# Attention of a diffusion trunk: two units' value products as one interleaved set, the probability copy placed first on ScalarE, filler products in two more branches

## The reference

```python
# A: two maps for each head, latent queries see 512 latent and 128 cached context keys
s = einsum(q, k) * scale ; p = softmax(s)
p = p[:, :, 0] - lam * p[:, :, 1] ; out = p @ v
# B: window of 128 around the query among the latent keys, plus 128 context keys, and a sink
p = exp(s - m) / (sum(exp(s - m)) + exp(sink - m)) ; out = p @ v
# C, D: one softmax over all 640 keys (C: 64-wide heads, D: 96-wide heads)
```

## Time and profile before

| what | us |
| --- | --- |
| median of three runs | 5234.26 |
| the profiled execution's own time | 5237.16 |
| its span | 5235.3 |
| attention of layer 1, first score product to last value product | 256 |
| PE busy in the whole span | 5096.8 (97%) |
| DVE busy | 3237.9 (62%) |
| ACT busy | 1682.5 (32%) |
| mean granted clock of PE | 0.986 |

### The profile page before, as it was taken

One profiled execution on the slowest core, in us unless ns is written; L12 is line 12 of the kernel. 1 busy time (PEld: TensorE's weight loads), 2 busy tenths in 40 slices (PEclk: granted clock), 3 DMA queues, 4 the chain that ended last, 5 costly groups with the idle time before them and its releaser, 6 DMA issues.

```text
span 5235.3 us, 68750 instructions
## 1 busy us (share of the span) xinstructions
PE 5096.8 (97%) x25730; PEld 4123.0 (79%) x25730; DVE 3237.9 (62%) x7229; ACT 1682.5 (32%) x2618; POOL 1268.3 (24%) x826
## 2 busy tenths in 40 slices
PE   7999999999999999999999999999999999999999
PEld 4666887788888888888876668868888888888887
DVE  3865211149899876666648652111698998666666
ACT  3344321333333332222233442213333333322222
POOL 1300221224434421111113002202344434111111
PEclk9989999999999999999999899999999999999999
DMA  7100121456787788888820001211577787888886
GB/s 281 34 26 1 48 73 60 189 206 220 264 282 253 246 310 290 290 290 290 288 76 29 26 1 55 70 60 61 205 253 242 268 280 238 319 289 289 289 290 222
DMA packets 349898, 982.01 MB, mean 188 GB/s; under 512 B 31648, under 2 KB 101408, under 8 KB 346272
## 3 DMA queue, kind: packets, MB, share of 16 engines
q1 hardware_dynamic: 216000, 553.19, 31.7%
q0 software_dynamic: 74880, 276.86, 15.3%
q10 hardware_dynamic: 58720, 148.04, 7.2%
HBM read 829.43 MB, written 148.54 MB: 187 GB/s over the span
## 4 chain that ended last, share of the span: by engine, by line
PE 85%; DVE 8%; DMA 2%; ACT 2%; issue 1%; DVEq 1%; ACTq 0%; POOL 0%; POOLq 0%; SPq 0%
PE PS L925 27%; PE PS L882 23%; PE PS L502 14%; PE PS L491 5%; PE PS L906 4%; PE PS L645 3%; PE PS L673 3%; DVE AR L1319 2%; PE PS L657 1%; PE PS L492 1%; PE PS L615 1%; DVE AR L1340 1%; DVE SM L1358 1%; DMA gates_by_expert<-AR 1%; PE PS L828 0%
## 5 line engine op out<-in xcount | busy, mean ns | idle before, releaser
L925 PE MATMUL PS<-HB,VR 128*128 128x512 f32 x6144 | 1394.8, 389 | 3.4 <-DVE HB L1619 3.4
L925 PEld LDWEIGHTS PS<-HB,VR 128*128 128x128 f32 x6144 | 1154.1, 188 | 244.9 <-issue 5.0
L882 PE MATMUL PS<-HR,UR 128*128 128x512 f32 x4128 | 1008.0, 398 | 0.0
L1662 POOL TENSOR_TENSOR UR<-WR,UR 128x1024 fp32r<-128x1024 f32 x212 | 529.5, 2499 | 1822.5 <-ACT UR L1125 945.7
L502 PE MATMUL PS<-HR,UR 128*128 128x320 f32 (+1 forms) x5952 | 914.2, 312 | 14.0 <-DVE HR L1294 9.7
L502 PEld LDWEIGHTS PS<-HR,UR 128*128 128x128 f32 x5952 | 877.3, 188 | 44.4 <-issue 27.4
L882 PEld LDWEIGHTS PS<-HR,UR 128*128 128x128 f32 x4128 | 764.3, 189 | 165.7
L1606 DVE TENSOR_TENSOR VR<-HT,VR 128x1024 fp32r<-128x1024 f32 x256 | 313.7, 1226 | 455.9 <-ACT VR L1244 368.1
L1244 ACT CAST VR<-HT 128x1024 fp32r<-128x1024 f32 x256 | 268.8, 1050 | 960.1 <-PE PS L925 955.9
L882 PE MATMUL PS<-HR 128*128 128x512 f32 x2016 | 486.6, 394 | 0.0
L882 PEld LDWEIGHTS PS<-HR 128*128 128x128 f32 x2016 | 372.1, 188 | 73.5
(11 more groups left out here) (201 smaller groups left out, 6076.4 us busy)
## 6 DMA issues: line engine op xcount, KB each, us to landing
WR<-in_uT SPq DMA_DIRECT2D x256, 512.0 KB
HT<-in_vtab SPq DMA_DIRECT2D x256, 512.0 KB, 4.6
activations<-AR ACTq DMA_DIRECT2D x256, 256.0 KB
gates_by_expert<-AR ACTq DMA_DIRECT2D x128, 512.0 KB, 3.6
HW<-activations SPq DMA_DIRECT2D x256, 256.0 KB
WR<-gates_by_expert SPq DMA_DIRECT2D x64, 1024.0 KB
AR<-in_ada SPq DMA_DIRECT2D x40, 1024.0 KB, 7.6
WR<-in_wgate SPq DMA_DIRECT2D x64, 640.0 KB, 3.9
```

The source lines that it names most:

```text
L882: last = pe.matmul(bank(n % 2), u_part(n, w)[:, c, :], HR[:, h, c, 0:LAT], start=c == 0 and i == 0, stop=c == DC - 1 and i == 2)
L925: last = pe.matmul(bank(d), VR[:, m % 4, w, P * d:P * d + P], HB[:, (m + 1) % 3, h, :], start=m == 0 and i == 0, stop=m == E1 - 1 and i == 2)
L1662: nc.gpsimd.tensor_tensor(dst, src, high.bitcast(F32), ALU.subtract).then_inc(sem_, 1)
```

## The change

1. `weigh` now takes a pair of units, in every second step from s = 4 on. It waits for both copies and interleaves the products: for each key tile one product into output rows 0 to 63 and one into rows 64 to 127. The number of products is the same.
2. PT has four places instead of two, and lies in the memory of UR. The copy of unit u waits for the products of the pair to which unit u-4 belongs.
3. In ACT's step the copy of unit s-2 stands ahead of the exponentials of unit s.
4. The unread product of 256 columns ahead of a turning is issued in branches A, B and C. It was issued in A alone.

```diff
--- before.py
+++ after.py
@@ -159,6 +159,9 @@
 
         XT = sb("XT", [P, DC, TOK])
         HT = sb("HT", [P, DC, TOK])
+        with nc.sbuf_tensor("turned_probs", [P, 4 * D], F32) as TP:
+            pass
+
         UR = sb("UR", [P, 2, 2, D], F32R)
         WR = sb("WR", [P, RING, SLOT])
         CN = sb("CN", [P, C_ALL])
@@ -235,7 +238,7 @@
         MODR = Arena(AR, AF - 512 * SETS, AF).take(SETS, 512)
         t_ = Arena(AR, shared, AF)
         PB = t_.take(3, 2, 640)
-        PT = t_.take(2, 640)
+        PT = TP[:, 0:4 * 640].rearrange("p (a b) -> p a b", a=4)
         u_ = Arena(AR, shared, AF)
         HSQ, HSTD, HRS = u_.take(2, TOK), u_.take(2, TOK), u_.take(2, TOK)
         g_ = Arena(AR, 0, shared)
@@ -650,28 +653,33 @@
                 br, j, t, hh = units[u]
                 if u >= 1:
                     pe.wait_ge(pt_ready, l * NU + u)
-                    if br == "A":
+                    if br != "D":
                         pe.matmul(bank(4, 256), ones, CN[:, 0:256], start=True, stop=True)
                 pe.wait_ge(p_ready, l * NU + (u + 1))
                 for i in range(len(key_tiles(br, t))):
                     last = pe.transpose(PF[:, 2048 + P * i:2048 + P * i + P], PB[:, u % 3, 0, P * i:P * i + P], ident)
                 last.then_inc(t_ready, 1)
 
-            def weigh(l, u):
-                br, j, t, hh = units[u]
-                h = 2 * j + hh
-                pe.wait_ge(pt_ready, l * NU + (u + 1))
-                if hh == 0 and u >= 4:
-                    pe.wait_ge(o_done, l * (NU // 2) + (u // 2 - 1))
-                v = {"A": lambda kt: VT[:, kt, 64 * h:64 * h + 64],
-                     "B": lambda kt: VT[:, kt, 256 + 64 * (h // 2):320 + 64 * (h // 2)],
-                     "C": lambda kt: VT[:, kt, 384 + 64 * (h // 2):448 + 64 * (h // 2)],
-                     "D": lambda kt: VD[:, kt, 64 * h:64 * h + 64]}[br]
+            def weigh(l, pair):
+                br, j, t, _ = units[2 * pair]
+                pe.wait_ge(pt_ready, l * NU + 2 * (pair + 1))
+                if pair >= 2:
+                    pe.wait_ge(o_done, l * (NU // 2) + (pair - 1))
+
+                def v(kt, hh):
+                    h = 2 * j + hh
+                    if br == "D":
+                        return VD[:, kt, 64 * h:64 * h + 64]
+                    at = {"A": 64 * h, "B": 256 + 64 * (h // 2), "C": 384 + 64 * (h // 2)}[br]
+                    return VT[:, kt, at:at + 64]
+
                 tiles = key_tiles(br, t)
-                out = PF[64 * hh:64 * hh + 64, 3072 + 512 * (u // 2 % 2):3072 + 512 * (u // 2 % 2) + P]
+                at = 3072 + 512 * (pair % 2)
                 for i, kt in enumerate(tiles):
-                    last = pe.matmul(out, v(kt), PT[:, u % 2, P * i:P * i + P], start=i == 0, stop=i == len(tiles) - 1)
-                last.then_inc(pv_done, 1)
+                    for hh in range(2):
+                        last = pe.matmul(PF[64 * hh:64 * hh + 64, at:at + P], v(kt, hh), PT[:, (2 * pair + hh) % 4, P * i:P * i + P],
+                                         start=i == 0, stop=i == len(tiles) - 1)
+                last.then_inc(pv_done, 2)
 
             pe.wait_ge(c_in, 32)
             pe.wait_ge(cs_ready, 1)
@@ -777,8 +785,8 @@
                         keep_busy(5, 2)
                     if 2 <= s < NU + 2:
                         turn(l, s - 2)
-                    if s >= 3:
-                        weigh(l, s - 3)
+                    if s >= 4 and s % 2 == 0:
+                        weigh(l, (s - 4) // 2)
                 keep_busy(5, 5)
                 phase_end(pe, l, 2)
 
@@ -1031,10 +1039,10 @@
             def turned(l, u):
                 br, j, t, hh = units[u]
                 act.wait_ge(t_ready, l * NU + (u + 1))
-                if u >= 2:
-                    act.wait_ge(pv_done, l * NU + (u - 1))
+                if u >= 4:
+                    act.wait_ge(pv_done, l * NU + 2 * ((u - 4) // 2 + 1))
                 n = P * len(key_tiles(br, t))
-                nc.scalar.copy(PT[:, u % 2, 0:n], PF[:, 2048:2048 + n]).then_inc(pt_ready, 1)
+                nc.scalar.copy(PT[:, u % 4, 0:n], PF[:, 2048:2048 + n]).then_inc(pt_ready, 1)
 
             def modulation_rows(l, which):
 
@@ -1110,10 +1118,10 @@
                 act.dma_start(st_kr[l], KR[0:D_ROPE, NEWK:KEYS]).then_inc(st_out, 16)
                 act.dma_start(st_v[l], VT[:, 5, :]).then_inc(st_out, 16)
                 for s in range(NU + 4):
+                    if 2 <= s < NU + 2:
+                        turned(l, s - 2)
                     if s < NU:
                         exps(l, s)
-                    if 2 <= s < NU + 2:
-                        turned(l, s - 2)
                     if s >= 4 and (s - 4) % 2 == 1:
                         heads(l, (s - 4) // 2)
                 def high_gate(i, k):
```

## The result

The changed kernel takes 5253.78 us (median of five, 5253.68 to 5258.11) against 5230.54 (median of five, 5227.63 to 5241.33): 1.0036 times the time, 95% interval 1.0021 to 1.0050. That is slower by 0.36%, with an interval that excludes no change; +23 us where +22 was forecast. The profiled execution took 5253.68 with a span of 5251.9, 16.6 more than before.

The account below looks back on a forecast made before the run. PE, 85% of the span, was taken to bound the kernel. Per layer A +31, B -9, C -1 and D -10 gave +11, so +22 for two layers: 5257 us against 5234.3, range 5208 to 5288.

Parts of the forecast that it names:

- The chain in A: From exponentials through scores, unread product, turning and copy to the next exponentials, closing in one step: 5.04 us against 4.03.
- the count at the full clock: Branch A with no low clock: twelve latent steps 1.0 us longer, two others 0.7 each, +13.5 us a layer.
- The clock in A: PE idle about 1.6 us every second step of A, so two thirds of A at the lower clock, 22 us a layer.
- The pairs side by side: Twenty value products of two latent units run in one unit's 1.24 us instead of 2.48, gaining 9.9 us a branch.
- the second rival: Pairs do not run side by side and stay at 2.48 us: +40 us a layer, 5314 us; chance 0.07.
- D: Branch D: pairing shortens it with nothing added, ACT and DVE not binding; -10 us a layer, bounds 0 and -12.
- B: Branch B: unread products hold the clock up and pairs save PE work; -9 us a layer, bounds -13 and 0.
- C: Branch C: unread products cost 10.8 us, pairing gives 9.9 back, copy waits go; -1 a layer, bounds -4 and +10.
- The copy's new place outside A: In B, C and D the chain spans two steps, 2.1 us each: free in C and D, removing waits in B.
- The sum: All four branches together: 31 - 9 - 1 - 10 = +11 us a layer, +22 for two layers.
- A's term: Branch A's share of the forecast, from the longer chain and the low clock: +31 us a layer.
- The first rival: The clock stays high in A: -13 us a layer, -26 in all, 5208 us; chance 0.28.

Follow-up runs that it names:

- the filled kernel: The changed kernel with three more unread products of 256 columns behind the turning in A's odd steps: 5222.96 us, ratio 0.9964.
- the fastest one: Changed kernel with old order and unpaired value products in A, no unread product in C, three in three steps of A: 5183.17 us, ratio 0.9897.
- the run of the pairs alone: The kernel before with paired value products and four buffers, old order, unread products in A alone: 5280.90 us, ratio 1.0078.

## Why the prediction was right, and where its steps were not

**The chain in A: right.** 4.86 us at the full clock, in the runs with the order alone and with the filled gap, against the 5.04 of the terms (I had let copy and exponentials follow without their overlap of 0.1, seen at 313.25 + 0.69 against 313.83), and 7.06 at the low one against 7.1. Taking a term of 0.54 out shortened it by 0.48. The idle time of PE, "about 1.6", measured 1.57, but the terms give 4.14 - 2.66 = 1.48. The order alone made A 14.3 longer in layer 1, where the count at the full clock had 13.5.

**The clock in A: right in kind, its cause only half named.** I had two thirds of A low; the clocks 0.73 and 0.69 are 54% and 62%. A was 24.5 and 26.2 us longer against my 31, because of this and because the kernel before had itself 24% low. I had counted its low stretch around 340 alone, but its clock is low at the start of A too, from about 293 to 303:

```profile
296.00:299.00 3.00, 3.00 (x9) 1.37 (x8) 1.65 (x3) 0.64 (x1) 0.00 (x0) 0.50 0.51 174
```

A low clock at the start stands in the changed kernel's trace and in the fastest one's too, and is all that is left of it there. I tied the fall to the order. The run with the order alone had 0.86 and 0.80, the one with pairs and the old order 0.74: the pairs lower the clock most.

**"The value products lie in the time between turning and next scores and are free here, so pairing brings A nothing": the step that failed.** Free they were, but as PE's work in that gap they held the clock. With pairs every second step lost them. By the order alone A is 96.6, by the pairs alone (with the old order and unread products everywhere) 91.7, by both 106.7: about 14, 9 and 24 over 82.3, nearly a sum. (One of six stretches of A with pairs and the old order, in the run of the pairs alone, took 86.6; the others took 91.5 to 91.7.)

**The pairs side by side: right.** 1.24 for twenty products; the second rival falls. What the Trainium skill says of weight loads (TensorE: Matmul & The Clock Gate, Part 3: Packing small matmuls), that they overlap running products only where the row group differs, would by my estimate have left 2.48; the trace does not agree and shows half of that, with 64-wide weights.

**D: mis-sized.** -10 expected, -7.5 measured: behind steps without value products PE waits for DVE's division, five times 0.31 in full steps and 1.17, 1.17 and 0.75 at the context units, 4.6 us in all. In the D of the kernel before no wait of PE ended with DVE. I had named DVE as not binding by its busy time, 29.3 of 58, which says nothing of a wait in a short step. **B** was -11.1 where I took -9, since the low clock of A was not handed on; **C** -2.0 for -1.

**The copy's new place outside A: right in sign, far too small.** I counted it as removing some waits. The run with pairs and the old order shows that the pairs depend on it: 13 us in B, 4 in C, 6 in D.

**The sum** was +11 a layer; attention shows +3.9 and +5.6. A's term was 5 to 7 too large; B, C and D add up to -20.5 against my -20. So attention gives 9.6 us for both layers, under half of the forecast. Another 7 lie outside attention, where the profiles wander by up to 13 us between the two layers' attentions alone, with no relation to the edits. The last 7 of the medians' +23 come of the profiled execution of before having been that far over its median (5237.2 against 5230.5), and no trace shows where. (5259 less 2.9 is 5256, not 5257.) The sign and the mechanism are shown, the closeness of 22 to 23 is largely luck. The first rival, a high clock in A, is nearly what the filled kernel shows: 18 us under the kernel before, where I had 26 under it.

## What to carry to other kernels

Before a wait is moved ahead of other work in an engine's list, follow the ring of waits that it closes between the two engines and count over how many steps it runs: in the kernel with pairs the same move was worth 13 us in B, where a unit has one map, and cost 15 in A, where it has two. When work is taken off TensorE, look at what the step without it looks like; here gains came only where the thin steps were filled, with waits gone or with unread products. Where the clock is high without them, unread products only cost: 7.3 us in C. And a choice that pays in one branch can be written for that branch alone: order, pairing and filling by branch gave a kernel 43 us under the one before (5241.0 to 5197.9), and filling three more thin steps brought that to 57 (5240.4 to 5183.2).

## What the runs showed of the hardware

TensorE's granted clock in attention went to 1.2 GHz in stretches in which it showed as busy for some nine tenths: 83.2 of 91.7 us with pairs and the old order at a mean of 0.74, and 51.6 of 58.8 at 0.71 in B without unread products. What preceded the falls were steps with products missing or with scores waiting on exponentials, not a long idle time: behind the branch's start, where PE waited 2.4 to 2.7 us, the longest gap in A was 1.57 us after the change and 0.94 with pairs and the old order. A fall outlived its branch, C's mean being 0.81 behind a low B and 1.00 with the same code behind a high one. Two interleaved groups of ten products, with weights of 64 columns and 128 columns streamed, ran in 1.24 us, the time of one group.
